# Zeros instead of x1 as the start of the scattered sums, and loads that add in the last norm

## The chip, the cores and the metric

One NeuronCore of one Trainium2 chip runs the whole program. The metric is the device time of one launch in microseconds; several launches are timed and the median is given. One of them was recorded by the hardware profiler.

## The reference

A single decoder layer is applied to 512 prompt tokens and 8 sample tokens (520 rows of 2048 float32 values, computed together). What matters here is the shape of the residual stream:

```python
x = layer_norm(ALPHA * x + mix, ln1_g[l], ln1_b[l])          # called x1 below
ffn = hier_moe(x, w_group[l], b_group[l], w_router[l], b_router[l],
               w_gate[l], w_up[l], w_down[l])
x = layer_norm(ALPHA * x + ffn, ln2_g[l], ln2_b[l])          # the output
...
# hier_moe: best of 4 groups, best 2 of its 4 experts, so two experts of 16 for each token
h = jax.nn.silu(jnp.einsum('td,edf->tef', xf, w_gate)) * jnp.einsum('td,edf->tef', xf, w_up)
y = jnp.einsum('tef,te,efd->td', h, gate.astype(h.dtype), w_down)
```

`mix` is the output of three groups of heads (short convolution, HGRN2 recurrence, windowed attention) behind one input projection and one output projection. An expert has three matrices of 4 MiB each: gate and up of 2048x512, down of 512x2048.

## The kernel before, in words

The program is written engine by engine, each with its own instruction list and explicit semaphores; nothing reorders it. It has these stages, in order of time in the profile:

- **Input projection and heads**, to about 600 us, and **output projection** (16 columns of w_out, `n` in 0 to 15), about 607 to 804 us. SP issues the loads: two 1 MiB buffers (`RAW`) hold weights, ScalarE copies them to a rounded high part (`HI`), GpSimd or VectorE makes the low part (`LO`), TensorE runs three products for each (high x high, low x high, high x low).
- **First norm and routing**, about 804 to 835 us. x1 lies in the tile `R` (104 rows of 5 token tiles, 2048 columns). SP writes it to `x1_rows` in HBM, from which GpSimd gathers the rows of each block of up to 128 (token, expert) pairs. The trace shortens the names `x1_rows` to `x_rows`, `X2` and `X8` to `X`, `LG2` to `LG`, `LB2` to `LB`.
- **Expert blocks**, about 835 to 1456 us. Each block takes 12 weight tiles of 1 MiB: eight for gate and up (`gate_up`, tiles 0 to 7) and four for down (`down`, tiles 8 to 11). SP issues a tile's load into one of six buffers `RAWB` once VectorE has finished the low part (`LOB`) of the tile that had the buffer (semaphores `expert_lo`). ScalarE then makes `HIB`, VectorE `LOB`, TensorE multiplies. The block's result `YO` is scattered by GpSimd to `y_rows` in HBM by an indirect DMA that adds (line 768). The blocks in the middle are a hardware loop on each engine; the first block and the last two stand outside it. In the last block but one, w_down is taken in four columns, and each quarter of `YO` is scattered alone (line 804). The last block's result stays on the chip (`YO2`): TensorE spreads it with 0/1 matrices over the token tiles.
- **Last norm**, from 1455 us. SP waits for the four quarter scatters, loads `y_rows` into `X2` (four tiles of 128 tokens, 1 MiB each, line 707) and the eight sample rows into `X8` (64 KiB, line 709). VectorE adds the spread last block (`added`, line 1767), centres and scales (`centred`, `finished`), ScalarE makes means and squares. The samples go another way through `samples_sum`, `samples_centre` and `samples_finish`, which stand between the tiles in VectorE's list. Tiles 0 and 1 of the output are written by GpSimd DMAs that add to rows already holding the bias (line 817); tiles 2 and 3 and the samples by SP.

`y_rows` must hold x1 before the first block is scattered, so that x1 and all blocks sum there. In the kernel before SP writes the five pieces of `R` to it in the first block's `gate_up`, one between every two weight loads from tile 3 on:

```python
def y_set(i):
    sp.dma_start(y_rows[i * TT:(i + 1) * TT, :], R[:, i, :]).then_inc(s_y0, 16)
...
if isinstance(j, int) and 3 <= i < 3 + NT:
    y_set(i - 3)
```

All loads and stores issued by SP share one hardware DMA queue (q1) and are worked off in the order of issue; GpSimd's go through the software queue (q0). Both use the same 16 DMA engines.

Of the kernel before, what the change touches and what calls it, by code (L numbers as in the profile page):

```python
# [11 lines left out]
ALU = mybir.AluOpType  # L12
# [5 lines left out]
SEQ, DB = 512, 8  # L18
# [24 lines left out]
EARLY = 3  # L43
CHUNKS = list(range(11)) + [12, 13, 11, 14, 15]
# [70 lines left out]
def build(nc, a, o):  # L115
# [149 lines left out]
    with ExitStack() as ctx:  # L265
# [219 lines left out]
        def passed(eng):  # L485

            eng.sem_inc(s_passed, 1)
# [3 lines left out]
        def _(sp):  # L491
# [113 lines left out]
            for n in range(KC):  # L605
# [20 lines left out]
                if n == 0:  # L626
                    sp.dma_start(IOS[0:TT, :], a["ios"]).then_inc(s_rc, 16)
                    sp.dma_start(IOS[TT:128, :], a["ios"][0:128 - TT, :]).then_inc(s_rc, 16)
                if n == 2:
                    sp.wait_ge(s_ob, 2)  # L630
                    sp.wait_ge(s_ym, 2 * EARLY)
                    sp.dma_start(R[0:3, 0:4, 1536:2048], a["ln1g"][0:3, :].rearrange("r (q n) -> r q n", q=4)).then_inc(s_lg, 16)
                    sp.dma_start(R[3:5, 0:4, 1536:2048], a["ln1b"][0:2, :].rearrange("r (q n) -> r q n", q=4)).then_inc(s_lg, 16)
# [24 lines left out]
            def y_set(i):  # L658
                sp.dma_start(y_rows[i * TT:(i + 1) * TT, :], R[:, i, :]).then_inc(s_y0, 16)

            def gate_up(j, m0):
                e = sp.value_load(EBI[0:1, bass.ds(j, 1)], min_val=0, max_val=NE - 1)
                for i in range(8):
                    if isinstance(j, int) and i == 1:
                        x1_out(3)
                        x1_out(4)
                    if isinstance(j, int) and 3 <= i < 3 + NT:
                        y_set(i - 3)
                    bload(i, m0, (a["w_gate"], a["w_up"])[i % 2][bass.ds(e, 1), :, 2048 * (i // 2):2048 * (i // 2) + 2048].rearrange("a p n -> p (a n)"), j)

            def down(j, first, columns=False):
                e = sp.value_load(EBI[0:1, bass.ds(j - 1, 1)], min_val=0, max_val=NE - 1)
                for n in range(4):
                    if columns:
                        w, parts = a["w_down"][bass.ds(e, 1), :, :, 512 * n:512 * n + 512].rearrange("a p c n -> p (a c) n"), 4
                    else:
                        w, parts = a["w_down"][bass.ds(e, 1), :, 2 * (n % 2):2 * (n % 2) + 2, 1024 * (n // 2):1024 * (n // 2) + 1024].rearrange("a p c n -> p (a c) n"), 1
                    i = first + n
                    s = i % NRAW
                    sp.wait_ge(b_lo[(2 + i) % NHL], (2 + i) // NHL + 1 + 4 * (j - 1))  # L680
                    passed(sp)
                    sp.dma_start(RAWB[:, s, :].rearrange("p (c n) -> p c n", c=parts), w).then_inc(b_raw[s], 16)
# [7 lines left out]
            gate_up(nb - 1, 0)  # L690
# [8 lines left out]
            sp.wait_ge(s_y0, 16 * NT)  # L699
# [4 lines left out]
            sp.wait_ge(b_yw, 16 * nb + 48)  # L704
            passed(sp)
            for i in range(NF):
                sp.dma_start(X2[:, i, :], y_rows[128 * i:128 * i + 128, :]).then_inc(f_in[i], 16)
            in8 = "(g r) (c n) -> (r c) g n"
            sp.dma_start(X8[:, :, :], y_rows[SEQ:T, :].rearrange(in8, g=2, c=32)).then_inc(f_in8, 16)
# [3 lines left out]
            sp.wait_ge(f_in8, 32)  # L713
# [13 lines left out]
        def _(pool):  # L727
# [53 lines left out]
            with pool.Fori(1, MAXB) as j:  # L781
                with pool.If(j < last):
# [5 lines left out]
                    pool.wait_ge(s_y0, 16 * NT)  # L788
# [12 lines left out]
            for n in range(4):  # L801
# [5 lines left out]
                    bounds_check=last_quarter, oob_is_err=False, compute_op=ALU.add).then_inc(b_yw, 16)  # L807
            pool.memset(ROWS[:, :], 0.0).then_inc(s_ones, 1)
# [370 lines left out]
        def _(dve):  # L1179
# [282 lines left out]
            lo(NU + 1)  # L1462

# [279 lines left out]
            def samples_sum():  # L1743
                dve.wait_ge(f_in8, 48)
# [622 lines left out]
```

## Time and profile before

| | |
|---|---|
| median of 3 launches | 1496.84 us (1494.42 to 1501.94) |
| profiled execution: device time | 1493.46 us |
| profiled execution: span of its instructions | 1491.6 us |
| mean granted TensorE clock | 0.982 of full speed |
| TensorE matmuls busy | 1439.3 us (96%) |
| VectorE busy | 1015.0 us (68%) |
| ScalarE busy | 770.8 us (52%) |
| GpSimd busy | 190.4 us (13%) |
| DMA moved | 335.36 MB, mean 225 GB/s |
| of it by the software queue q0 | 18.74 MB, 5.0% of 16 engines' span |

Engines are named PE (TensorE matmuls), PEld (its weight loads), DVE (VectorE), ACT (ScalarE), POOL (GpSimd) and SP (SyncE, which only issues DMAs; its queue rows say SPq). A number after L is the line in the kernel. Times of rows are microseconds from the start of the span, durations in "mean ns" nanoseconds.

### The profile page before, as it was taken

Reading aid. Unit: us, or ns where it says so; the run is one execution under the profiler, and the core shown is the slowest. Engines: PE = TensorE matmul, PEld = TensorE weight load, DVE = VectorE, ACT = ScalarE, POOL = GpSimd, SP = SyncE. Lnnn points to the kernel's source line nnn. Section 1 sums busy time; section 2 is a strip of 40 time slices with the busy share of each in tenths; the row PEclk is TensorE's granted clock in tenths of the full one; section 3 lists DMA queues with packets and bytes.
Section 4 is the critical chain, followed back from the end, with each engine's and each line's share of the span. In section 5 each row is a group of like instructions: output and inputs, shape, how many; then the busy total and the mean of one; then the engine's idle time right before and its main releaser. Section 6 shows DMA issues by size and latency. Waiting matters only on the chain.

```text
span 1491.6 us, 24267 instructions
## 1 busy us (share of the span) xinstructions
PE 1439.3 (96%) x9396; PEld 1291.7 (87%) x9396; DVE 1015.0 (68%) x1287; ACT 770.8 (52%) x912; POOL 190.4 (13%) x99
## 2 busy tenths in 40 slices
PE   8999999999999999999997999999999999999995
PEld 7999999999999999999996467888888888888772
DVE  4246746757777787523125668888888888888877
ACT  4245545444434433411110047777777777777774
POOL 0000000000000000234330001121121211222130
PEclk9999999999999999999998899999999999999998
DMA  7321231322213312633435699999999999999997
GB/s 262 123 89 57 86 114 61 96 90 86 88 57 115 116 58 73 205 111 146 145 96 205 207 394 375 384 401 391 392 375 384 384 382 398 387 390 401 348 294 232
DMA packets 74389, 335.36 MB, mean 225 GB/s; under 512 B 12086, under 2 KB 18790, under 8 KB 45514
## 3 DMA queue, kind: packets, MB, share of 16 engines
q1 hardware_dynamic: 68842, 315.54, 56.2%
q0 software_dynamic: 5472, 18.74, 5.0%
q8 instruction: 56, 0.92, 0.2%
q14 instruction: 19, 0.16, 0.0%
HBM read 313.56 MB, written 40.73 MB: 238 GB/s over the span
## 4 chain that ended last, share of the span: by engine, by line
PE 85%; DVE 7%; DMA 3%; ACT 2%; issue 2%; POOL 0%; ACTq 0%; SPq 0%; DVEq 0%; POOLq 0%
PE BANK L1811 13%; PE BANK L1812 13%; PE BANK L1813 13%; PE BANK L2170 7%; PE BANK L2172 7%; PE BANK L2171 7%; PE BANK L2222 4%; PE BANK L2220 4%; PE BANK L2221 4%; PE BANK L2154 2%; DMA RAWB<-in_w_up 2%; PE BANK L2183 2%; PE BANK L1953 1%; PE BANK L1829 1%; PE BANK L2050 1%
## 5 line engine op out<-in xcount | busy, mean ns | idle before, releaser
L1811 PE MATMUL BANK<-XH,HI 128*128 128x260 f32 x1746 | 503.0, 288 | 1.4 <-DVE RT L1487 1.0
L1683 DVE TENSOR_TENSOR LOB<-RAWB,HIB 128x2048 fp32r<-128x2048 f32 x196 | 448.6, 2291 | 74.0 <-ACT HIB L1050 73.1
L1812 PE MATMUL BANK<-XL,HI 128*128 128x260 f32 x1746 | 495.3, 284 | 0.0
L1813 PE MATMUL BANK<-XH,LO 128*128 128x260 f32 x1746 | 494.3, 283 | 0.0
L1050 ACT ACTIVATE HIB<-RAWB 128x2048 fp32r<-128x2048 f32 x196 | 376.4, 1921 | 86.0 <-PE BANK L2172 66.1
L1811 PEld LDWEIGHTS BANK<-XH,HI 128*128 128x128 f32 x1746 | 331.2, 190 | 2.7 <-issue 1.7
L1812 PEld LDWEIGHTS BANK<-XL,HI 128*128 128x128 f32 x1746 | 331.1, 190 | 0.7
L1813 PEld LDWEIGHTS BANK<-XH,LO 128*128 128x128 f32 x1746 | 330.9, 190 | 0.0
L2170 PE MATMUL BANK<-HIB,XGH 128*128 128x512 f32 x512 | 201.8, 394 | 5.5 <-issue 3.0
L2172 PE MATMUL BANK<-LOB,XGH 128*128 128x512 f32 x512 | 200.0, 391 | 0.0
L2171 PE MATMUL BANK<-HIB,XGL 128*128 128x512 f32 x512 | 199.8, 390 | 0.0
L836 ACT ACTIVATE HI<-RAW 128x2048 fp32r<-128x2048 f32 x55 | 105.1, 1911 | 146.5 <-PE BANK L1813 139.6
L731 POOL TENSOR_TENSOR LO<-RAW,HI 128x2048 fp32r<-128x2048 f32 x14 | 66.1, 4721 | 713.5 <-ACT HI L836 713.5
L1198 DVE TENSOR_TENSOR LO<-RAW,HI 128x2048 fp32r<-128x2048 f32 x41 | 93.8, 2289 | 42.9 <-ACT HI L836 42.6
L2170 PEld LDWEIGHTS BANK<-HIB,XGH 128*128 128x128 f32 x512 | 96.7, 189 | 26.2 <-DVE LOB L1683 3.3
L2172 PEld LDWEIGHTS BANK<-LOB,XGH 128*128 128x128 f32 x512 | 96.5, 188 | 20.5
L1487 DVE SCALAR_TENSOR_TENSOR RT<-RT,BANK 128x260 f32<-128x260 f32 x32 | 13.5, 424 | 147.3 <-PE BANK L1813 147.3
L2171 PEld LDWEIGHTS BANK<-HIB,XGL 128*128 128x128 f32 x512 | 96.6, 189 | 19.5
L2220 PE MATMUL BANK<-HIB,HTH 128*128 128x512 f32 x240 | 99.4, 414 | 0.0
L2222 PE MATMUL BANK<-LOB,HTH 128*128 128x512 f32 x240 | 94.7, 395 | 0.0
L2221 PE MATMUL BANK<-HIB,HTL 128*128 128x512 f32 x240 | 93.6, 390 | 0.0
L768 POOL DMA_INDIRECT y_rows<-YO,YIXC x15 | 37.4, 2495 | 355.3 <-ACT YO L1071 355.3
(388 smaller groups left out, 1674.5 us busy)
## 6 DMA issues: line engine op xcount, KB each, us to landing
RAWB<-in_w_down SPq DMA_DIRECT2D x68, 1024.0 KB, 9.5
RAWB<-in_w_gate SPq DMA_DIRECT2D x67, 1024.0 KB, 9.4
RAWB<-in_w_up SPq DMA_DIRECT2D x67, 1024.0 KB, 8.9
RAW<-in_w_in SPq DMA_DIRECT2D x39, 1024.0 KB, 4.9
RAW<-in_w_out SPq DMA_DIRECT2D x16, 1024.0 KB, 5.0
Y<-in_xT SPq DMA_DIRECT2D x8, 520.0 KB, 9.1
RT<-in_xT SPq DMA_DIRECT2D x16, 260.0 KB, 5.2
x_rows<-R SPq DMA_DIRECT2D x5, 832.0 KB
```

What stands on the lines that cost most here:

```text
L836: act.activation(HI[:, u % 2, :], RAW[:, u % 2, :], ACT.Copy).then_inc(s_hi, 1)
L1050: act.activation(HIB[:, s, :], RAWB[:, r, :], ACT.Copy).then_inc(b_hi, 1)
L1683: dve.tensor_tensor(LOB[:, s, :], RAWB[:, r, :], HIB[:, s, :].bitcast(F32), ALU.subtract).then_inc(b_lo[s], 1)
L1811: pe.matmul(bank, hw[:, c, :], h, start=(c == 0), stop=False)
L1812: pe.matmul(bank, hw[:, c, :], l, start=False, stop=False)
L1813: ins = pe.matmul(bank, lw[:, c, :], h, start=False, stop=(c == KC - 1))
L2170: pe.matmul(b, XGH[:, cc, :], hw[:, c, :], start=(cc == 0), stop=False)
L2171: pe.matmul(b, XGL[:, cc, :], hw[:, c, :], start=False, stop=False)
L2172: ins = pe.matmul(b, XGH[:, cc, :], lw[:, c, :], start=False, stop=(cc == KC - 1))
L2220: pe.matmul(b, th[:, c, :], hw[:, m, :], start=(c == 0), stop=False)
L2221: pe.matmul(b, tl[:, c, :], hw[:, m, :], start=False, stop=False)
L2222: ins = pe.matmul(b, th[:, c, :], lw[:, m, :], start=False, stop=(c == 3))
```

## The change

Five things change.

1. `y_rows` starts at zero. VectorE clears the tile `NDIST` (128x256, no longer used by then) at the start of the output projection, and SP writes it, repeated eight times along a row, to the five pieces of `y_rows` at n = 3, 4, 8, 12 and 13. The five writes of x1 in the first block go.
2. In the last `gate_up` SP loads x1 from `x1_rows` into `X2`, one tile of 1 MiB before weight tiles 0, 2, 4 and 6, and after tile 7 the sample rows into `X8`.
3. After the quarter scatters GpSimd, no longer SP, issues the loads of `y_rows` into `X2` and `X8`, now as DMAs that add to what is there.
4. Waits follow: scatters wait for the zeros, `samples_sum` for the adding load of `X8`.
5. The w_down loads that are not in columns name their destination as 2 pieces of 1024 instead of 1 of 2048.

```diff
+ZEROED = (3, 4, 8, 12, 13)
...
+                if n in ZEROED:
+                    i = ZEROED.index(n)
+                    sp.wait_ge(s_y0, 1)
+                    sp.dma_start(y_rows[i * TT:(i + 1) * TT, :].rearrange("p (k c) -> p k c", c=256),
+                                 NDIST[0:TT, :].unsqueeze(1).to_broadcast([TT, 8, 256])).then_inc(s_y0, 16)
...
-            def y_set(i):
-                sp.dma_start(y_rows[i * TT:(i + 1) * TT, :], R[:, i, :]).then_inc(s_y0, 16)
-
-            def gate_up(j, m0):
+            def x1_in(i):
+                if i == 0:
+                    sp.wait_ge(s_x1w, 16 * (5 + NT))
+                sp.dma_start(X2[:, i, :], x1_rows[128 * i:128 * i + 128, :]).then_inc(s_y0, 16)
+
+            def gate_up(j, m0, fill=False):
...
-                    if isinstance(j, int) and 3 <= i < 3 + NT:
-                        y_set(i - 3)
+                    if fill and i % 2 == 0:
+                        x1_in(i // 2)
...
-                        w, parts = a["w_down"][bass.ds(e, 1), :, 2 * (n % 2):2 * (n % 2) + 2, 1024 * (n // 2):1024 * (n // 2) + 1024].rearrange("a p c n -> p (a c) n"), 1
+                        w, parts = a["w_down"][bass.ds(e, 1), :, 2 * (n % 2):2 * (n % 2) + 2, 1024 * (n // 2):1024 * (n // 2) + 1024].rearrange("a p c n -> p (a c) n"), 2
...
-            gate_up(nb - 1, 0)
+            gate_up(nb - 1, 0, True)
+            sp.dma_start(X8[:, :, :], x1_rows[SEQ:T, :].rearrange(in8, g=2, c=32)).then_inc(s_y0, 16)
             down(nb - 1, 8, True)
             down(nb, 0, True)
...
-            sp.wait_ge(s_y0, 16 * NT)
...
-            sp.wait_ge(b_yw, 16 * nb + 48)
-            passed(sp)
-            for i in range(NF):
-                sp.dma_start(X2[:, i, :], y_rows[128 * i:128 * i + 128, :]).then_inc(f_in[i], 16)
-            in8 = "(g r) (c n) -> (r c) g n"
-            sp.dma_start(X8[:, :, :], y_rows[SEQ:T, :].rearrange(in8, g=2, c=32)).then_inc(f_in8, 16)
...
-            sp.wait_ge(f_in8, 32)
+            sp.wait_ge(f_in8, 16)
...
-                    pool.wait_ge(s_y0, 16 * NT)
+                    pool.wait_ge(s_y0, 1 + 16 * NT)
...
+            pool.wait_ge(b_yw, 16 * nb + 48)
+            passed(pool)
+            pool.wait_ge(s_y0, 1 + 16 * (NT + NF + 1))
+            pool.wait_ge(b_xg, 16 * last)
+            passed(pool)
+            for i in range(NF):
+                pool.dma_start(out=X2[:, i, :], in_=y_rows[128 * i:128 * i + 128, :], accum_op=ALU.add).then_inc(f_in[i], 16)
+            pool.dma_start(out=X8[:, :, :], in_=y_rows[SEQ:T, :].rearrange(in8, g=2, c=32), accum_op=ALU.add).then_inc(b_xg, 16)
             pool.memset(ROWS[:, :], 0.0).then_inc(s_ones, 1)
...
             lo(NU + 1)
+            dve.memset(NDIST[:, :], 0.0).then_inc(s_y0, 1)
...
             def samples_sum():
-                dve.wait_ge(f_in8, 48)
+                dve.wait_ge(f_in8, 32)
+                dve.wait_ge(b_xg, 16 * nb)
```

How the program's order moves is seen at two places. The first is SP's list in the last `gate_up`, outside the loop; the kernel before:

```order
L662 TENSOR_LOAD EBI
L662 ISA x2
L600 ISA
L602 ISA [waits expert_lo2]
L602 DMA RAWB<-in_w_gate 128x2048
L600 REGISTER_ALU
L602 DMA RAWB<-in_w_up 128x2048 [waits expert_lo0]
L602 ISA [waits expert_lo1]
L602 DMA RAWB<-in_w_gate 128x2048
```

and the changed one (X2 is the tile of the last norm, the names carry the changed kernel's lines):

```order
L672 ISA x2
L669 DMA X2_118<-x1_rows 128x2048 [waits x1_out]
L601 ISA
L603 ISA [waits expert_lo2]
L603 DMA RAWB_94<-in_w_gate 128x2048
L601 REGISTER_ALU
L603 DMA RAWB_94<-in_w_up 128x2048 [waits expert_lo0]
L669 DMA X2_118<-x1_rows 128x2048
L603 ISA [waits expert_lo1]
L603 DMA RAWB_94<-in_w_gate 128x2048
```

A load of x1 now stands in SP's queue ahead of weight tile 0 and ahead of tile 2, and two more ahead of tiles 4 and 6.

The second is GpSimd's list behind the quarter scatters, the kernel before:

```order
L804 DMA y_rows<-YO,YIX_171 2080x512 [waits down_copied]
L808 MEMSET ROWS 128x128
L811 MEMSET ROWS 32x32 [waits ones_set]
L811 MEMSET ROWS 32x32 x3
L817 DMA out_yp<-YA 128x2048 [waits tokens_in,y_scaled,y_out]
L817 DMA out_yp<-YA 128x2048 [waits y_scaled]
```

and the changed one:

```order
L808 DMA y_rows<-YO,YIX4_171 2080x512 [waits down_copied]
L813 ISA
L819 DMA X2_118<-y_rows 128x2048 [waits block_out,y_rows_set,tokens_in]
L819 DMA X2_118<-y_rows 128x2048 x3
L820 DMA X8_119<-y_rows 128x2x64
L821 MEMSET ROWS_123 128x128
L824 MEMSET ROWS_123 32x32 [waits ones_set]
L824 MEMSET ROWS_123 32x32 x3
L830 DMA out_yp<-YA_111 128x2048 [waits tokens_in,y_scaled,y_out]
```

Five DMAs come into GpSimd's list between the last scatter and the clearing of `ROWS`, and stand in the software queue ahead of the two output writes.

## Rows read from the trace of the kernel before

**Rows 1.** The page's chain that ended last: share of the span by engine.
```profile
PE 85%; DVE 7%; DMA 3%; ACT 2%; issue 2%; POOL 0%; ACTq 0%; SPq 0%; DVEq 0%; POOLq 0%
```

**Rows 2.** Stages: length, busy of PE, PEld, DVE, ACT, POOL; clock, DMA share, GB/s.
```profile
740.00:760.00 20.00, 20.00 (x171) 20.00 (x170) 5.12 (x10) 1.92 (x1) 9.02 (x2) 1.00 0.28 96
855.00:870.00 15.00, 15.00 (x33) 5.59 (x32) 8.89 (x6) 5.37 (x4) 0.00 (x0) 1.00 1.02 399
1000.00:1100.00 100.00, 100.00 (x469) 83.55 (x469) 88.65 (x53) 79.14 (x65) 17.19 (x11) 1.00 1.00 385
1405.00:1410.00 5.00, 2.03 (x12) 1.62 (x10) 3.13 (x3) 4.88 (x5) 0.00 (x0) 1.00 0.86 306
1410.00:1415.00 5.00, 5.00 (x22) 4.13 (x23) 2.97 (x3) 2.04 (x2) 0.00 (x0) 1.00 0.80 311
1415.00:1420.00 5.00, 5.00 (x23) 4.13 (x22) 4.50 (x2) 3.87 (x3) 2.50 (x1) 1.00 0.81 248
```

**Rows 3.** SP's queue in the first block: start, us, what it issued.
```profile
868.03 0.55 SPq L659 DMA_DIRECT2D y_rows<-R  x1
869.77 0.34 SPq L602 DMA_DIRECT2D RAWB<-in_w_up  x1
```

**Rows 4.** ScalarE and TensorE in the first block: start, us, what, idle before.
```profile
894.02 1.92 ACT L1050 ACTIVATE HIB<-RAWB 128x2048 fp32r<-128x2048 f32 x1 [3.13 <-DMA RAWB<-in_w_up]
...
898.32 0.50 PE L2170 MATMUL BANK<-HIB,XGH 128*128 128x512 f32 x1 [1.28 <-DVE LOB L1683]
```

**Rows 5.** TensorE at 608 us, and VectorE's clearing of a 128x512 tile.
```profile
607.89 0.36 PE L1811 MATMUL BANK<-XH,HI 128*128 128x260 f32 x1 [1.03 <-DVE RT L1487]
...
L1302 DVE MEMSET SF<- 128x512 f32 x4 | 1.9, 485 | 0.6 <-DVE PR L1387 0.5
```

**Rows 6.** SP's queue in the last gate_up: tiles 0, 3, 5, 6, 7 and 8.
```profile
1390.11 0.35 SPq L602 DMA_DIRECT2D RAWB<-in_w_gate  x1
...
1395.30 0.33 SPq L602 DMA_DIRECT2D RAWB<-in_w_up  x1
...
1402.18 0.33 SPq L602 DMA_DIRECT2D RAWB<-in_w_up  x1
1405.52 0.33 SPq L602 DMA_DIRECT2D RAWB<-in_w_gate  x1
1409.45 0.33 SPq L602 DMA_DIRECT2D RAWB<-in_w_up  x1
1414.41 21.17 SPq L682 DMA_DIRECT2D RAWB<-in_w_down  x8
```

**Rows 7.** DMA issues of 1395-1396, 1402-1403, 1416-1419: count, size, us to landing.
```profile
RAWB<-in_w_up SPq DMA_DIRECT2D x1, 1024.0 KB, 8.4
...
RAWB<-in_w_up SPq DMA_DIRECT2D x1, 1024.0 KB, 6.9
...
RAWB<-in_w_down SPq DMA_DIRECT2D x1, 1024.0 KB, 7.7
```

**Rows 8.** ScalarE in the last gate_up: tiles 2, 5, 6, and 7 to 9.
```profile
1407.46 1.93 ACT L1050 ACTIVATE HIB<-RAWB 128x2048 fp32r<-128x2048 f32 x1
...
1418.40 1.92 ACT L1050 ACTIVATE HIB<-RAWB 128x2048 fp32r<-128x2048 f32 x1 [0.80 <-PE BANK L2172]
1421.18 1.92 ACT L1050 ACTIVATE HIB<-RAWB 128x2048 fp32r<-128x2048 f32 x1 [0.86 <-PE BANK L2172]
1426.16 5.53 ACT L1050 ACTIVATE HIB<-RAWB 128x2048 fp32r<-128x2048 f32 x3 [3.06 <-issue]
```

**Rows 9.** The chain of waits at the end: start, us, what.
```profile
1446.28 8.68 DMA y_rows<-YO,YIX
...
1455.04 4.85 DMA X<-y_rows
1459.92 2.53 DVE X L1767 x8
...
1473.01 0.30 DVE X L1745
...
1487.31 0.29 DVE Q L1760
```

**Rows 10.** DMA queues in 1473-1481.8 and 1460-1463: packets, MB, share of 16 engines.
```profile
q0 software_dynamic: 189, 1.42, 89.0%
...
q1 hardware_dynamic: 175, 1.30, 102.7%
```

**Rows 11.** GpSimd's first adding write of the output.
```profile
1473.00 0.93 POOL L817 DMA_DIRECT2D out_yp<-YA  x1 [23.75 <-ACT YA L1161]
```

**Rows 12.** GB/s in 40 equal slices of 1473 to 1475 us.
```profile
GB/s 0 0 0 0 0 0 0 0 0 0 0 0 0 0 0 0 0 0 0 0 0 0 0 0 0 0 0 0 0 164 983 983 328 164 0 0 0 0 0 0
```

More of the change, by code:

```diff
@@ L656, in _ @@
                 x1_out(i)
-            def y_set(i):
-                sp.dma_start(y_rows[i * TT:(i + 1) * TT, :], R[:, i, :]).then_inc(s_y0, 16)
-            def gate_up(j, m0):
+            in8 = "(g r) (c n) -> (r c) g n"
+            def x1_in(i):
[3 more added lines that the diff above has]
+            def gate_up(j, m0, fill=False):
                 e = sp.value_load(EBI[0:1, bass.ds(j, 1)], min_val=0, max_val=NE - 1)
@@ L807, in _ @@
                     bounds_check=last_quarter, oob_is_err=False, compute_op=ALU.add).then_inc(b_yw, 16)
+            in8 = "(g r) (c n) -> (r c) g n"
+            pool.wait_ge(b_yw, 16 * nb + 48)
[6 more added lines that the diff above has]
+            pool.dma_start(out=X8[:, :, :], in_=y_rows[SEQ:T, :].rearrange(in8, g=2, c=32), accum_op=ALU.add).then_inc(b_xg, 16)
             pool.memset(ROWS[:, :], 0.0).then_inc(s_ones, 1)
```

## The prediction

> **What bounds the kernel now.** I read the page's chain first [rows 1]: TensorE holds 85% of it, VectorE 7%, DMA 3%. A change that touches neither TensorE's list nor its operands can only act where TensorE or the last norm waits. Then the table of stages [rows 2]. In the middle expert blocks (1000 to 1100) TensorE is busy 100.00 of 100 us while the DMA share is 1.00 at 385 GB/s: TensorE sets the pace, but the DMA engines have next to nothing to spare, so bytes put into or taken out of the expert stage matter at its ends, where TensorE has gaps. In the output projection (740 to 760) the share is 0.28 at 96 GB/s, so there is room. Then the queues and engines at three places: the first block, the last `gate_up`, and the end.
>
> In the first block the DMA engines are full (share 1.02 at 399 GB/s in 855 to 870 [rows 2]). The last x1 write to `y_rows` is issued at 868.03 and tile 7 right after, at 869.77 [rows 3]. ScalarE waits 3.13 us for that tile, until 894.02, and TensorE in turn stands 1.28 us before 898.32 [rows 4]. That is all the time TensorE loses there to the DMA queue. At the end the chain is: last quarter scatter 8.68 us, first load of `y_rows` 4.85 us, then VectorE nearly without a break from 1459.92 to 1487.6, then the last store [rows 9].
>
> **The change part by part.** Times are of the profiled execution: span 1491.6, device time 1493.5 us, 3.4 us under the median of 1496.84 (all three launches lie within 1494.4 to 1501.9). I add the sum to both.
>
> *x1 writes of the first block go.* Five writes, 520 x 8 KB = 4.26 MB. At 399 GB/s [rows 2] that is 10.7 us of queue ahead of tile 7. The tile would land about 11 us earlier, well before ScalarE wants it, and the 1.28 us gap closes. Nothing behind it gains more, since TensorE has no idle time in the blocks that follow. The first scatter also need not wait for them, but it waits for the block's result anyway. Gain 1.3 us, at least 1.0. The other end is a case in which the whole 10.7 us comes back; it is a rival below.
>
> *Zeros.* The memset of `NDIST` stands in VectorE's list just ahead of the residual addition for which TensorE waits 1.03 us until 607.89 [rows 5]. A 128x512 memset took 485 ns, so half of that size is about 0.24 us, and I put it on the path: +0.2, bounds 0 and 0.5. The five writes cover again 4.26 MB, in 1 KB pieces, in a stage where the engines are busy 0.28 of the time [rows 2]: 4.26 MB at half of 399 GB/s would be 21 us spread over 120 us or more. TensorE is busy 20.00 of 20 us there, so its weight tiles come in time, and I take 0; if that cover failed, one late weight tile would cost about 3 us.
>
> *x1 loads in the last block.* Four tiles of 1 MiB come into SP's queue ahead of weight tiles 0, 2, 4 and 6, and 64 KB behind tile 7. Two landings give the pace of the queue: tile 3 was issued at 1395.30 and took 8.4 us, tile 5 at 1402.18 and took 6.9 [rows 6, 7]: they land at 1403.7 and 1409.1, so 2.7 us for each tile. Tiles 0 and 1 then land 2.7 us later, 2 and 3 5.4, 4 and 5 8.1, 6 and 7 10.8. Against that stands how early they are now. Tile 2 lands near 1401.0 and is used at 1407.46, 6.5 us of slack against 5.4. Tile 5 has 1418.40 - 1409.1 = 9.3 against 8.1 [rows 8]. Tile 6 follows tile 5 by two tiles in the new queue (one of x1, its own): 1409.1 + 8.1 + 5.4 = 1422.6, and it is used at 1421.18, so 1.4 us late. The wait is not made up, because ScalarE then leaves its loop with 3.06 us of its own ("issue") before tile 7 at 1426.16 [rows 8], and that tile is what TensorE waits for. The w_down tiles inherit what is left of the 10.8 us. The engines were idle for 0.14, 0.20 and 0.19 of three stretches of 5 us [rows 2], 2.7 us in all, so 8.1 us is left. A w_down tile issued about 1417.4 took 7.7 us, to 1425.1 [rows 7], and was used as the third of ScalarE's row at about 1429.8 [rows 8]: 4.7 us of slack, plus the 1.4 already lost, so about 2 us more. These overlap in part; I take +2.5 us for TensorE's end. Bounds: 0 (all hidden) and 10.8 (nothing hidden); I hold to the low side because each slack was read off.
>
> *The quarter scatters* run while SP's queue still works off that backlog; now the last takes 8.68 us [rows 9] beside the gamma and beta loads, which come later in the changed kernel. +0.5, bounds 0 and 3.
>
> *Adding loads.* The load of `y_rows` moves to GpSimd. SP issued 0.08 us after the scatter landed (1446.28 + 8.68, to 1455.04) [rows 9]; GpSimd has two more waits to pass and an issue of 0.93 us [rows 11], of which +0.4 shows. The rate matters more. The trace has a direct DMA that adds only in the other direction, from SBUF to HBM (line 817). Issued at 1473.00 [rows 11], its first packets are in the 30th of 40 slices of 0.05 us, at 1474.45 [rows 12], and alone in the machine until SP's first store at 1481.8 it moved 1.42 MB [rows 10]: 193 GB/s, 5.4 us for 1 MiB. Plain loads into `X2` moved 1.30 MB in 3 us at a share of 1.03 [rows 10]: 422 GB/s of full engines, 2.5 us for 1 MiB. So an adding load into SBUF costs between 2.5 and 5.8 us a tile (1.42 MB over 0.89 of 8.8 us gives the 5.8); the nearest row is the adding one and I take 5.4. The first plain tile landed 4.85 us after its issue [rows 9], 2.4 more than its 2.5 of moving. Adding tiles then land 2.4 + 5.4 = 7.8, 13.2, 18.6 and 24.0 us after the first issue, and the 64 KB of samples, in 256-byte pieces, about 2 us later, 26. Before, VectorE started tile 0 at 4.9, tile 1 at 10.1, the sample sum at 1473.01 - 1455.04 = 18.0. Now tile 0 starts 2.9 us late, tile 2 5.7 late, and `samples_sum`, which stands ahead of tile 3 in VectorE's list, 8.0 late. Everything behind it (tile 3, three centrings, two finishes, the samples' finish, the last store) follows it without slack. So +8.0, bounds 0 and 9.5. GpSimd's own adding stores stand in q0 behind these loads: 26 + 2 x 5.4 = 37 after the issue, and the end is then at 36.6 + 8, so they are covered.
>
> The Trainium skill bears on the direction that no row has. "Collectives: The Full Stack", section "The bandwidth ceiling: the fold count and why AG ≠ RS ≠ AR", says that a DMA that adds is slower not for the adding but because it must read two sources for one write, and gives a ratio of 1.93. That holds for any direction, so it speaks against plain speed here. By that rule a tile would take 1.93 x 2.5 = 4.8 us as an estimate and the sample sum would start 5.6 us late instead of 8.0, the whole 2.4 us sooner than my sum. This trace has 5.4 / 2.5 = 2.2 for writes to HBM [rows 10], and nothing for loads.
>
> *w_down's two pieces.* The source was two pieces of 1024 per partition already; the loads lie in blocks where TensorE is never idle [rows 2]. 0.
>
> Sum: -1.3 + 0.2 + 2.5 + 0.5 + 0.4 + 8.0 = +10.3 us. Profiled device time 1503.8, median 1507.
>
> **The rivals.** (a) *Adding loads run at the plain pace.* At 2.5 us a tile they land at 4.9, 7.4, 9.9 and 12.4, the samples before 15, all ahead of VectorE's 18.0; the 8.0 goes to 0 and the sum is +2.3: 1499, no measurable change. For it: a write into SBUF has no HBM row to read back. Against it: each byte is still read twice. It decides at 18.0 = 2.4 + 4t + 2, that is t = 3.4 us a tile; above that the end moves. (b) *The x1 loads are not hidden at all.* Tiles 6 and 7 late by their full 10.8 us: 8.3 more than I count, 1515. For it: share 1.00 in the loop and no spare for the first tiles. Against it: the 6.5 and 9.3 us of slack. (c) *The start gives back all it carried.* If the 10.7 us of writes held the whole expert stage back, taking them out would give 10.7, and with plain-speed loads the sum is 2.3 - (10.7 - 1.3) = -7.1, with the last block hidden too -9.6: 1488. Against it: TensorE's 100% in rows 2, which leaves an earlier DMA nothing to bring forward. (d) *The zero writes hold up SP.* Pieces of 1 KB at n = 12 and 13 delay a w_out tile or the first expert tiles: 3 us on top, 1510.
>
> **How the numbers follow.** Chances: forecast 0.53, (a) 0.27, (b) 0.11, (c) 0.05, (d) 0.04. A measurement of this kernel tells about 0.5%, 7.5 us, from no change, so the line is at 1504.3. The forecast's own range is 1501 to 1511: with 4.8 us a tile and TensorE's delay at 1 it falls just under the line; I count 0.1 of its 0.53 as the same. (b) and (d) are slower. So slower 0.58, same 0.37, faster 0.05. The range runs from (a) with the last block hidden, 1497, to (b), 1515.
>
> **What would show it.** In the profile after: no wait of ScalarE for tile 7 and no TensorE gap near 896 (else the first step is wrong); a DMA share over 1 in the last `gate_up`, ScalarE starting tile 6 one to three us late and TensorE's end two to three us later relative to its start of that block; the first adding load landing nearly 8 us after its issue, and VectorE idle before tile 2 and above all before the sample sum. If VectorE goes from tile 0 to tile 3 without waits for DMA, the forecast is wrong and (a) is right. If TensorE is idle in the middle blocks, either kernel's DMA pace decides and I misread the stage.

## The result and the profile after

| | before | changed |
|---|---|---|
| median of 9 launches each | 1496.85 us (1493.87 to 1501.94) | 1503.57 us (1499.88 to 1506.92) |
| ratio, 95% interval | | 1.0044 [1.0032, 1.0056] |
| profiled span | 1491.6 us | 1501.4 us |
| mean granted TensorE clock | 0.982 | 0.981 |

The changed kernel is 6.6 us slower (4.8 to 8.4). The profiled pair differs by 9.8 us, so some of what one pair of traces shows is not the change; the experiments below take the parts one by one.

The chain by engine, from the page of the changed kernel:

```profile
PE 84%; DVE 7%; DMA 4%; ACT 3%; issue 2%; POOL 0%; ACTq 0%; POOLq 0%; SPq 0%; DVEq 0%
```

Against [rows 1] TensorE's share is down by one point and DMA's and ScalarE's are up by one each. One point is 15 us, so this only says that some waiting came in. The queues, from the same page:

```profile
DMA packets 78878, 339.62 MB, mean 226 GB/s; under 512 B 12423, under 2 KB 23287, under 8 KB 50011
...
q0 software_dynamic: 6320, 23.00, 6.4%
```

The kernel moves 4.26 MB more in all (335.36 before): the x1 loads. It moves 4.26 MB more in the software queue (18.74 before): the loads that went over to GpSimd.

**The start.** VectorE and TensorE at 609 us, timeline of the changed kernel (start, us, engine, what, in brackets the idle time before and who ended it):

```profile
606.97 2.28 DVE L1211 TENSOR_TENSOR LO<-RAW,HI 128x2048 fp32r<-128x2048 f32 x1
609.26 0.27 DVE L1476 MEMSET NDIST<- 128x256 f32 x1
609.85 0.76 DVE L1501 SCALAR_TENSOR_TENSOR RT<-RT,BANK 128x260 f32<-128x260 f32 x2
...
610.42 0.36 PE L1826 MATMUL BANK<-XH,HI 128*128 128x260 f32 x1 [1.27 <-DVE RT L1501]
```

TensorE's wait for the residual addition is 1.27 us where it was 1.03 [rows 5]: the memset costs 0.24. The addition itself is 2.53 us later than before, but VectorE's item ahead of the memset is already 2.3 us later, so that part is from before the change. The stages of the changed kernel, with the zeros in flight in the first two rows (length, busy PE, PEld, DVE, ACT, POOL; clock, DMA share, GB/s):

```profile
600.00:700.00 100.00, 98.73 (x825) 98.55 (x824) 32.88 (x58) 24.21 (x23) 33.95 (x7) 0.98 0.56 189
700.00:800.00 100.00, 100.00 (x859) 100.00 (x858) 23.60 (x46) 13.42 (x7) 32.14 (x7) 1.00 0.40 132
...
880.00:885.00 5.00, 5.00 (x23) 4.11 (x22) 3.62 (x3) 3.56 (x3) 0.00 (x0) 1.00 0.52 166
```

The same two windows of the kernel before:

```profile
600.00:700.00 100.00, 98.97 (x828) 98.80 (x827) 30.98 (x54) 23.82 (x22) 33.95 (x7) 0.98 0.49 171
700.00:800.00 100.00, 100.00 (x863) 100.00 (x861) 23.17 (x45) 11.52 (x7) 32.14 (x7) 1.00 0.33 111
```

The zeros raise the DMA share from 0.49 and 0.33 to 0.56 and 0.40 and TensorE still has all of 100 us in the second window. In the first block the pressure is gone: the share is 0.52 at 880 to 885, where it was 0.94. ScalarE there, timeline after:

```profile
890.30 1.92 ACT L1063 ACTIVATE HIB<-RAWB 128x2048 fp32r<-128x2048 f32 x1 [0.80 <-PE BANK L2187]
...
895.68 1.92 ACT L1063 ACTIVATE HIB<-RAWB 128x2048 fp32r<-128x2048 f32 x1 [0.80 <-PE BANK L2187]
...
901.13 0.60 ACT L1072 ACTIVATE SG<-BANK 128x512 f32<-128x512 f32 x1 [0.81 <-PE BANK L2187]
```

It waits for TensorE now and no longer 3.13 us for a load [rows 4]. From the residual addition (`RT`, near 608 us, just behind the memset) to the silu `SG` near 901 us the changed kernel takes 901.13 - 609.85 = 291.3 us, the kernel before 294.1. I call this the start stretch.

**The last gate_up**, windows of the changed kernel:

```profile
1405.00:1410.00 5.00, 2.15 (x12) 1.68 (x10) 3.35 (x3) 5.00 (x6) 0.00 (x0) 1.00 1.01 421
1410.00:1415.00 5.00, 4.88 (x14) 3.90 (x15) 2.89 (x2) 0.60 (x2) 0.00 (x0) 0.66 1.02 424
1415.00:1420.00 5.00, 5.00 (x23) 4.13 (x22) 2.83 (x2) 3.82 (x3) 2.28 (x1) 1.00 1.01 423
```

The DMA share is 1.01 to 1.02 where it was 0.80 to 0.86 [rows 2]: the x1 loads fill the gaps. ScalarE and TensorE in it:

```profile
1410.12 0.49 PE L2185 MATMUL BANK<-HIB,XGH 128*128 128x512 f32 x1 [2.97 <-issue]
...
1414.50 1.92 ACT L1063 ACTIVATE HIB<-RAWB 128x2048 fp32r<-128x2048 f32 x1 [4.40 <-PE BANK L2187]
...
1423.01 1.92 ACT L1063 ACTIVATE HIB<-RAWB 128x2048 fp32r<-128x2048 f32 x1 [0.86 <-PE BANK L2187]
1427.99 5.52 ACT L1063 ACTIVATE HIB<-RAWB 128x2048 fp32r<-128x2048 f32 x3 [3.06 <-issue]
```

Every wait of ScalarE ends on TensorE or on its own sequence, none on a load. It starts tile 6 at 1423.01, against 1421.18 [rows 8], 1.83 us later, though the block started only 0.2 us later. The delay is there already at tile 3 (4.40 us of waiting for TensorE) and belongs to the granted clock of 0.66 in 1410 to 1415, which was 1.00 in the profile before: 0.34 of 5 us is 1.7 us lost for TensorE.

**The last norm**, timeline of GpSimd and VectorE after:

```profile
1458.60 3.56 POOL L819 DMA_DIRECT2D X<-y_rows  x4 [8.43 <-DMA y_rows<-YO,YIX]
1460.86 2.55 POOL L820 DMA_DIRECT2D X<-y_rows  x1
...
1466.66 0.69 DVE L1782 SCALAR_TENSOR_TENSOR X<-X,BANK 128x512 f32<-128x512 f32 x1 [11.34 <-DMA X<-y_rows]
1477.35 0.69 DVE L1782 SCALAR_TENSOR_TENSOR X<-X,BANK 128x512 f32<-128x512 f32 x1 [2.87 <-DMA X<-y_rows]
1484.31 0.29 DVE L1760 TENSOR_TENSOR X<-X,W 128x128 f32<-128x128 f32 x1 [2.10 <-DMA W<-z_rows]
```

and the DMAs in the chain that ended last (start, us, what):

```profile
1448.13 9.74 DMA y_rows<-YO,YIX
1458.60 8.03 DMA X<-y_rows
1471.51 8.22 DMA z_rows<-Z
1479.74 4.45 DMA W<-z_rows
```

Counted from the first issue at 1458.60, tile 0 starts at 8.1 us, tile 2 at 18.75, the sample sum at 25.7. In the profile before these were 4.9, 12.9 and 18.0 ([rows 9], and for tile 2 this line of the same chain), and VectorE went from tile to tile:

```profile
1467.98 2.53 DVE X L1767 x8
```

The whole tail, first issue to the end of the span, is 42.8 us, against 1491.6 - 1455.04 = 36.6 [rows 9]. DMA queues of 1466 to 1475, after (packets, MB, share of 16 engines):

```profile
DMA packets 261, 1.95 MB, mean 217 GB/s; under 512 B 23, under 2 KB 23, under 8 KB 23
...
q0 software_dynamic: 261, 1.95, 104.8%
```

and of 1456 to 1466 before, where the plain loads run:

```profile
DMA packets 535, 3.99 MB, mean 399 GB/s; under 512 B 48, under 2 KB 48, under 8 KB 48
...
q1 hardware_dynamic: 535, 3.99, 99.4%
```

Both fill the engines: the adding loads at 217 GB/s (187 in 1460 to 1466, at a share of 0.98), the plain ones at 399.

The 9.8 us of this pair lie at these places:

- The last `gate_up` starts 0.2 us later. 2.3 us were lost ahead of the first changed instruction and 0.2 at the memset; the rest was recovered in between.
- From there to the issue of the fourth quarter scatter: +1.6, its low clock.
- That scatter takes 9.74 us and not 8.68: +1.1.
- From its landing to the first issue it is 0.73 us and not 0.08: +0.65.
- The tail: +6.2.

### The profile page after: what moved, and what is told of

Its sections match the earlier page's. It is cut to its first block, busy times and chain, and to the rows that moved or that the text cites. A ratio compares the mean times of both kernels' runs of the same rounds, so it can differ in the third digit from the quotient of the medians.

```text
span 1501.4 us, 24275 instructions
## 1 busy us (share of the span) xinstructions
PE 1440.4 (96%) x9396; PEld 1292.4 (86%) x9396; DVE 1015.7 (68%) x1288; ACT 771.3 (51%) x912; POOL 195.2 (13%) x104
## 4 chain that ended last, share of the span: by engine, by line
PE 84%; DVE 7%; DMA 4%; ACT 3%; issue 2%; POOL 0%; ACTq 0%; POOLq 0%; SPq 0%; DVEq 0%
PE BANK L1826 12%; PE BANK L1827 12%; PE BANK L1828 12%; PE BANK L2185 7%; PE BANK L2187 7%; PE BANK L2186 7%; PE BANK L2237 4%; PE BANK L2235 4%; PE BANK L2236 4%; PE BANK L2169 2%; PE BANK L2198 2%; PE BANK L1968 1%; PE BANK L1844 1%; PE BANK L2065 1%; ACT SC L906 1%
```

## The experiments

Intervals are 95%, ratios always to the kernel before, whose median stayed between 1496.9 and 1498.5 us in all comparisons. "tail" and "start stretch" are measured as above; "PE stretch" is from TensorE's first matmul of the last `gate_up` to the issue of the fourth quarter scatter (before 36.4, changed 38.0 us).

**Zeros alone.** The kernel before, with the first part of the change only. Nothing loads x1 in its place, so x1 is missing from the last norm's input.

```diff
+                if n in ZEROED:
...
+                    sp.dma_start(y_rows[i * TT:(i + 1) * TT, :].rearrange("p (k c) -> p k c", c=256),
+                                 NDIST[0:TT, :].unsqueeze(1).to_broadcast([TT, 8, 256])).then_inc(s_y0, 16)
...
-                    if isinstance(j, int) and 3 <= i < 3 + NT:
-                        y_set(i - 3)
```

> Only the start of the change: zeros written during the output projection, the five x1 writes of the first block gone; no x1 loads, plain loads as before, so x1 is missing from the last norm's input. Theory P (the adding loads are the loss, the x1 writes cost only the gap at tile 7): 0.2 for the memset less 1.3 for the gap, so about 1 us faster than before, ratio 0.999; in the profile no TensorE gap near 896. Rival S (the x1 writes hold the whole expert stage back, and the change's loss at the end is far larger than its net): 5 to 10 us faster, ratio 0.994 to 0.997. Rival C (TensorE's clock drop in the first block comes from these writes): the drop after the block's start is gone in this profile, 1.5 us more.

Ratio 0.9982 [0.9968, 0.9995]: 2.7 us faster. No gap of TensorE is left in 880 to 905; start stretch 293.1 us in a trace with a clock of 0.94 and 0.97 in 860 to 900, so a low clock in the first block does not need the x1 writes. Tail 36.6, as before. Taking the x1 writes out gives more than the 1.1 us that the traced gap promised (1.3 less 0.2 for the memset), and far less than 10.7. The low clock at 1410 to 1415 is here too, without any x1 load:

```profile
1410.00:1415.00 5.00, 4.43 (x13) 3.63 (x14) 2.89 (x2) 0.51 (x2) 0.00 (x0) 0.66 0.76 264
```

**x1 loads alone.** The kernel before, with x1 loaded in the last `gate_up` and then overwritten by the plain loads.

```diff
+                    if fill and i % 2 == 0:
+                        x1_in(i // 2)
...
-            gate_up(nb - 1, 0)
+            gate_up(nb - 1, 0, True)
+            sp.dma_start(X8[:, :, :], x1_rows[SEQ:T, :].rearrange(in8, g=2, c=32)).then_inc(s_y0, 16)
```

> The kernel before plus the x1 loads of the last gate_up and nothing else (the plain loads of y_rows overwrite them later): the result is as before. Theory P: DMA share goes to 1.0 in 1405 to 1420, ScalarE waits for no tile, TensorE's end is unmoved; the last quarter scatter lands up to 1 us later; 0 to 1 us slower, ratio 1.000 to 1.001. Rival Q (the queue's backlog reaches TensorE): 2.5 us or more slower, ratio 1.002 or more, with ScalarE idle on DMA RAWB at tiles 6 to 9. Rival C2 (the fuller DMA queue brings the clock drop at the last block): a granted clock below 1 in 1410 to 1415.

Ratio 1.0019 [1.0008, 1.0031], profiled span 1503.5. But the trace puts nearly all of its extra time ahead of the place that was edited: start stretch 302.2 us against 294.1, with two gaps of TensorE:

```profile
900.45 0.50 PE L2180 MATMUL BANK<-HIB,XGH 128*128 128x512 f32 x1 [1.71 <-DVE LOB L1693]
905.46 0.50 PE L2180 MATMUL BANK<-HIB,XGH 128*128 128x512 f32 x1 [1.98 <-DVE LOB L1693]
```

and low clocks earlier, in stages where TensorE never stood, as in this window:

```profile
700.00:720.00 20.00, 20.00 (x154) 20.00 (x153) 7.29 (x13) 3.11 (x2) 4.59 (x1) 0.83 0.22 80
```

In the last `gate_up` the share is 1.00 to 1.02, ScalarE waits for no load, and the PE stretch is 38.0. Tail 36.8. The edit's own cost cannot be read from one trace like this; a second one follows below.

**Adding loads on top.** As above, with the five loads made adding ones of GpSimd. The sums in the last norm hold x1 twice.

```diff
-            for i in range(NF):
-                sp.dma_start(X2[:, i, :], y_rows[128 * i:128 * i + 128, :]).then_inc(f_in[i], 16)
...
+            for i in range(NF):
+                pool.dma_start(out=X2[:, i, :], in_=y_rows[128 * i:128 * i + 128, :], accum_op=ALU.add).then_inc(f_in[i], 16)
```

> e2 plus the adding loads issued by GpSimd, with the x1 writes of the first block kept (x1 is counted twice in the last norm's input). Theory P: 6 to 8 us slower than e2, so ratio 1.004 to 1.006 over before; the first adding load lands 8 us after its issue, the sample sum starts about 26 us after it. Rival R (the pace of the loads does not matter, the loss is in the queue ahead of them): within 1 us of e2.

Ratio 1.0058 [1.0044, 1.0071], so 0.0039 or 5.8 us over x1 loads alone in the same comparison. VectorE's waits:

```profile
1475.09 0.69 DVE L1782 SCALAR_TENSOR_TENSOR X<-X,BANK 128x512 f32<-128x512 f32 x1 [11.14 <-DMA X<-y_rows]
1487.00 0.69 DVE L1782 SCALAR_TENSOR_TENSOR X<-X,BANK 128x512 f32<-128x512 f32 x1 [4.09 <-DMA X<-y_rows]
1492.90 0.29 DVE L1760 TENSOR_TENSOR X<-X,W 128x128 f32<-128x128 f32 x1 [1.04 <-DMA X<-y_rows]
```

From the issue at 1467.05: 8.0, 19.95 and 25.85 us. Tail 42.95. Tile 0 and the samples come as in the changed kernel and tile 2 1.2 us later, with another start of the sums: the pace belongs to the kind of DMA.

**Plain loads by GpSimd.** The changed kernel, with `accum_op` taken from the five loads; the last norm then lacks x1.

```diff
-                pool.dma_start(out=X2[:, i, :], in_=y_rows[128 * i:128 * i + 128, :], accum_op=ALU.add).then_inc(f_in[i], 16)
+                pool.dma_start(out=X2[:, i, :], in_=y_rows[128 * i:128 * i + 128, :]).then_inc(f_in[i], 16)
```

> The changed kernel with the five loads of y_rows made plain, still issued by GpSimd (they overwrite x1, which is missing from the last norm's input). Theory P: the loads land at 2.5 us a tile, VectorE waits only for the first, and the kernel is about 6 us faster than the changed one: -1.3 + 0.2 + 0 to 1 + 0.6 for the issue, ratio 0.999 to 1.001 over before. Rival I (issue from GpSimd through the software queue is what costs, not the adding): the loads still land 15 us and more after issue, ratio 1.003 to 1.004.

Ratio 0.9997 [0.9984, 1.0010]. GpSimd and VectorE in it:

```profile
1458.53 2.23 POOL L819 DMA_DIRECT2D X<-y_rows  x4 [8.51 <-DMA y_rows<-YO,YIX]
...
1463.64 0.69 DVE L1782 SCALAR_TENSOR_TENSOR X<-X,BANK 128x512 f32<-128x512 f32 x1 [8.48 <-DMA X<-y_rows]
```

Tile 0 starts 5.1 us after the issue and the tail is 36.7, so the one argument `accum_op` of five DMAs carries 42.8 - 36.7 = 6.1 us by the traces and 0.0047 x 1497 = 7.0 us by the launches. Issue by GpSimd costs about 0.9: the issue comes 0.75 us after the scatter's landing (0.08 by SP) and the first load lands in 5.09 us (4.85). PE stretch 37.8, scatter 9.80 us.

**The kernel before against itself**, and **x1 loads again.** The kernel before and the kernel of "x1 loads alone" once more, with nothing changed.

> The kernel before, unchanged, timed against itself. All theories expect a ratio of 1.000 within 0.001; its width is what the others are read against. Theory K (the stretches of TensorE at its lower clock fall by the program's own course): its profile has the drops where the profile of before has them, in 860 to 880 and not in 1400 to 1420. Rival L (they fall by chance): a drop of the same length stands in another stage.

> e2 unchanged, a second time. In its first profile TensorE had further stretches at a lower clock in 700 to 720 and 900 to 920, hundreds of microseconds ahead of the only edit, and the kernel was 2.8 us slower. Theory K (by the program's course): the same two stretches again, ratio 1.002. Rival L (by chance): they are gone in this profile, ratio 1.000 to 1.001, since the x1 loads themselves cost TensorE nothing.

Ratios 0.9999 [0.9982, 1.0017] and 1.0004 [0.9989, 1.0019]. The new trace of the kernel before spans 1500.2 us, 8.6 more than the first, and has the gaps that the first lacked:

```profile
896.34 0.50 PE L2170 MATMUL BANK<-HIB,XGH 128*128 128x512 f32 x1 [1.80 <-DVE LOB L1683]
901.39 0.50 PE L2170 MATMUL BANK<-HIB,XGH 128*128 128x512 f32 x1 [2.03 <-DVE LOB L1683]
...
906.05 0.60 ACT L1059 ACTIVATE SG<-BANK 128x512 f32<-128x512 f32 x1 [2.02 <-PE BANK L2172]
```

Its start stretch is 297.4 us; x1 loads again has 296.9. And its clock has a low stretch where the first trace had none, and a longer one (windows):

```profile
900.00:905.00 5.00, 3.61 (x10) 2.86 (x11) 4.57 (x3) 3.41 (x2) 0.00 (x0) 0.73 0.97 387
...
1415.00:1420.00 5.00, 4.67 (x11) 3.71 (x12) 2.89 (x2) 0.32 (x1) 0.00 (x0) 0.50 0.83 308
```

So the first trace of the kernel before, on which the prediction rests, was one of its better executions: 294.1 us where the other four traces with the x1 writes at their old place (this one, the two of x1 loads, and x1 loads with adding loads) have 296.9 to 302.2. Its PE stretch was 36.4, and this second one's, under the longer low stretch, 39.1, with no x1 loads in either. The mean of the two comparisons for x1 loads is 1.0012, about 1.7 us, and one interval holds 1.

**x1 writes later.** The kernel before with its five writes moved behind the `w_down` loads, one before them and one after each of the four.

```diff
-                    if isinstance(j, int) and 3 <= i < 3 + NT:
-                        y_set(i - 3)
...
+                    if isinstance(j, int):
+                        y_set(n + 1)
...
+            y_set(0)
```

> The kernel before with its five x1 writes moved behind tile 7: one ahead of the first w_down tile, one behind each of the four. No zeros, no x1 loads, plain loads. Theory P (the writes cost only because they stand ahead of tiles that TensorE is about to want, and the engines are idle for 3 to 4 us in 880 to 890 without them): the gap at 896 goes and no new one of that size comes, 1 to 2 us faster, ratio 0.999. Rival M (the engines have no room anywhere in the first two blocks): the same gap comes back at the w_down tiles or in the second block, ratio 1.000 to 1.001.

Ratio 1.0000 [0.9982, 1.0017]. The gap at 896 goes, and the start stretch is 291.3 us, as in the changed kernel. But the block's scatter, which waits for the five writes, and the gather behind it are later: GpSimd's first item after that wait starts at 906.59 after 29.85 us of idling (891.86 before), and TensorE pays:

```profile
906.59 1.12 POOL L764 COPY YIXC<-YIX 128x1 int32 x1 [29.85 <-DMA y_rows<-R]
...
914.10 0.79 PE L2171 MATMUL BANK<-HIB,XGH 128*128 128x512 f32 x1 [2.74 <-DVE XGL L1694]
```

The gain is given back 13 us later. The writes cost something at both places tried in the full stage, and nothing was seen of them in the output projection.

**Samples behind tile 3.** The changed kernel with the sample sum moved behind the addition of tile 3 and the centring of tile 2.

```diff
+            added(3)
+            centred(2)
             samples_sum()
-            added(3)
+            finished(2, 1)
             samples_centre()
-            centred(2)
-            finished(2, 1)
```

> The changed kernel with the sample sum moved in VectorE's list from ahead of tile 3 to behind tile 3 and its centring. Theory P (the adding loads set the pace, the sample sum is only the last to come): VectorE starts tile 3 when it lands, 24 us after the first issue instead of 26.2, about 2 us faster than the changed kernel, ratio 1.002 to 1.004 over before. Rival W (the samples' own way, the write and read of the 64 KB of z_rows beside the adding loads, is what holds the end): the end comes with the samples and nothing is gained, or 1 us is lost.

Ratio 1.0034 [1.0019, 1.0049], tail 42.3 us. Tile 3 now starts 25.2 us after the first issue (at 1456.36), as soon as it has landed and no longer behind the samples (26.25 in the changed kernel):

```profile
1481.56 0.69 DVE L1782 SCALAR_TENSOR_TENSOR X<-X,BANK 128x512 f32<-128x512 f32 x1 [0.23 <-DMA X<-y_rows]
```

About 2 us were expected from the new order. It is worth 0.5 us of the 6.2 by the tails; by the launches the interval overlaps that of the changed kernel, so no gain is shown there. What binds is the pace of the four tiles: tile 3 lands 25 us after the issue and not 24.

**Half and half.** Zeros, x1 loads and adding loads only for tiles 2 and 3. Tiles 0 and 1 and the samples start from x1 and are loaded plainly by SP, so that VectorE has work while the adding loads run. Of the x1 writes 2.2 MB stay in the first block. Nothing is left out of the computation. The edit is shown against the changed kernel; w_down's loads name one piece here, as in the kernel before.

```diff
-ZEROED = (3, 4, 8, 12, 13)
+ZEROED = (3, 8)
...
-                    if fill and i % 2 == 0:
-                        x1_in(i // 2)
+                    if isinstance(j, int) and 3 <= i < 7:
+                        y_set(i - 3)
+                    if fill and i in (2, 4):
+                        x1_in(1 + i // 2)
...
+            for i in range(2):
+                sp.dma_start(X2[:, i, :], y_rows[128 * i:128 * i + 128, :]).then_inc(f_in[i], 16)
...
-            for i in range(NF):
+            for i in range(2, NF):
                 pool.dma_start(out=X2[:, i, :], in_=y_rows[128 * i:128 * i + 128, :], accum_op=ALU.add).then_inc(f_in[i], 16)
```

> A version of full result: only rows 256 to 511 of y_rows start at zero (tiles 2 and 3 of the last norm, x1 loaded into their place in the last gate_up, y added onto it by two GpSimd loads); rows 0 to 255 and the samples start at x1, written in the first block as before but 2.2 MB instead of 4.3, and are loaded plainly by SP. Theory P: VectorE wants tile 2 about 13 us and tile 3 about 18.5 us after the first load; two plain and two adding tiles land at about 13 and 18.5, so the end is lost by at most 1 us, and half of the writes ahead of tile 7 (5 us of queue) is enough to lose the gap at 896: 1 to 2.5 us faster than the kernel before, ratio 0.998 to 0.9995. Rival T (adding loads slow the plain loads beside them, and the sum is no better): VectorE waits for tile 1 or 3 by 2 us or more and the ratio is 1.000 to 1.002.

Ratio 1.0001 [0.9988, 1.0013]. The DMAs in its chain:

```profile
1458.05 5.10 DMA X<-y_rows
...
1468.02 8.52 DMA z_rows<-Z
1476.56 1.87 DMA W<-z_rows
```

and VectorE's waits:

```profile
1470.51 0.69 DVE L1790 SCALAR_TENSOR_TENSOR X<-X,BANK 128x512 f32<-128x512 f32 x1 [2.02 <-DMA X<-y_rows]
1478.46 0.29 DVE L1768 TENSOR_TENSOR X<-X,W 128x128 f32<-128x128 f32 x1 [0.27 <-DMA W<-z_rows]
```

VectorE waits for no load of tile 2 any more. But it now waits 2.0 us for plain tile 1, which runs beside the adding loads of the other queue. Behind that it waits 0.3 us for the samples, whose 64 KB write takes 8.5 us. The tail is 39.05, 2.5 us over that of the kernel before, which uses up what the start stretch of 291.3 gained.

**Three repeats**: half and half, zeros alone, and the changed kernel, with nothing changed.

> The same kernel a second time, since the width of one comparison is as large as the effect. Theory P: ratio 0.998 to 0.9995. Rival T: 1.000 to 1.002.

> e1 a second time (zero start alone, x1 missing from the last norm's input). Revised theory P2 (in the usual execution the x1 writes of the first block cost TensorE two gaps and not the one of the first profile): 3 us faster than the kernel before, ratio 0.998, no gap before 900. First theory: 1 us faster, ratio 0.999.

> The changed kernel a second time. Theory P2: 3 lost at the adding loads' 6 to 7 less 3 at the start and about 1 for the queue's last loads and the issue: ratio 1.003 to 1.005; first adding tile 8 us after its issue, sample sum 26 after it, and in the last block a TensorE that waits for no weight tile. Rival: these were of one execution, and the landings move by more than 1 us.

Ratios 0.9990 [0.9976, 1.0004], 0.9975 [0.9963, 0.9987] and 1.0042 [1.0027, 1.0058]. Tails 38.9, 36.7 and 42.9 us. Start stretches 293.3, 292.7 and 291.6. Half and half beats the changed kernel by some 7 us (means of two, 0.9996 and 1.0043), with intervals apart; against the kernel before it is not shown to differ. No version that computes everything was shown to beat the kernel before.

## Why the prediction was right, and where its sizes were not

The forecast was +10.3 us, a slower kernel because of the pace of the adding loads, and the launches say +6.6. The sign and the main cause were right; nearly every size was off, mostly towards too slow. Point by point:

| step | forecast | measured |
|---|---|---|
| x1 writes go | -1.3 | with the memset: -2.7 and -3.7 by launches (zeros alone, twice) |
| memset of the zeros | +0.2 | +0.24 (TensorE's wait 1.03 to 1.27) |
| the zeros' DMAs | 0 | 0 (TensorE 100.00 of 100 us at a share of 0.40) |
| x1 loads delay TensorE | +2.5 | no wait seen; by launches +1.7 as a mean, once not told from 0 |
| quarter scatter beside them | +0.5 | not resolved: 8.5 to 9.9 us in kernels with and without x1 loads |
| GpSimd starts the loads | +0.4 | +0.9 (0.67 to the issue, 0.24 in the landing) |
| adding loads | +8.0 | 6.1 by tails, 7.0 and 5.8 by launches |

*The adding loads, right in mechanism.* 7.8, 18.6 and 26 us from the issue were forecast for tile 0, tile 2 and the samples; 8.1, 18.75 and 25.7 were seen, and the wait stands where the prediction put it, before tile 2 and before the sample sum. Leaving out `accum_op` alone takes it away. The pace was taken from a row of the other direction, adding stores to HBM (5.4 us a tile), and comes near for loads: tile 2 lands 10.7 us after tile 0 here, 5.35 us a tile, and 11.9 in three other traces, 5.9 a tile. Against the 2.5 of plain loads that is 2.1 to 2.4 times as long; by the throughput of full engines the ratio is 1.8 to 2.1 (399 over 217 and 187 GB/s). The Trainium skill, "Collectives: The Full Stack", section "The bandwidth ceiling: the fold count and why AG ≠ RS ≠ AR", gives two reads for a write and a ratio of 1.93 for the adding step of a ring collective. The throughput measured here agrees with that ratio, the landings lie above it. The term itself was 1 to 2 us too large: `samples_sum` is late by 25.7 - 18.0 = 7.7 as forecast, but that is not all handed on to the end. From VectorE's last item to the end of the span the changed kernel takes 1501.4 - 1498.9 = 2.5 us and the kernel before 1491.6 - 1487.6 = 4.0: the sample store landed in 2.1 us there and in 3.6 before, where it stood with more stores under way (SP's two 512 KB stores landed in a median of 4.2 us before and 2.8 after). The step that let everything behind the sample sum, the last store too, follow it without slack was wrong by these 1.5 us.

*The start, too small.* "Gain 1.3 us" was read off one gap in one trace. That trace was one of the better executions. The other trace of the same kernel has two gaps, of 1.8 and 2.0 us, the three others with the x1 writes at their old place have two of 0.9 to 2.0, and a low clock may follow. The bound given, "at least 1.0", held; the size was half or less of what was measured. The reading that nothing beyond the gaps comes back was right: some 3 us and not 10.7.

*The last block, too large.* The prediction let tile 6 land 1.4 us late and stacked 8.1 us of backlog behind it. No wait of ScalarE for a load in this block appeared in any of the nine traces that have x1 loads there (two of them with half of the loads), though the engines ran full as forecast. The landings show the step that was too large. Tile 5 was to land at 1417.2; in the changed kernel it was issued at 1402.39 and took 13.1 us, so it landed at 1415.5. Tile 6's landing is on record in plain loads by GpSimd, first its issue and the time to landing, then ScalarE's start on it:

```profile
RAWB<-in_w_gate SPq DMA_DIRECT2D x1, 1024.0 KB, 15.0
...
1422.87 1.92 ACT L1063 ACTIVATE HIB<-RAWB 128x2048 fp32r<-128x2048 f32 x1 [0.86 <-PE BANK L2187]
```

Issued at 1406.10, it landed at 1421.1, 1.8 us before it was used. Most of that margin comes from the low clock, which holds TensorE and with it ScalarE back. At full clock, in the kernel before, ScalarE took tile 6 11.3 us after TensorE's first product of the block (1421.18 - 1409.90). Here the tile landed 10.9 us after it (1421.1 - 1410.18), in x1 loads alone and with adding loads on top 11.1 and 11.2. So at full clock it would have been in time by 0.1 to 0.4 us, as an estimate: hidden, but barely. The pace is the reason. From tile 2's landing at 1406.2 to tile 5's at 1416.1 four tiles pass, 2.5 us each, where the prediction took 2.7 from two landings of a queue that was not always full.

The sign given in advance, "ScalarE starting tile 6 one to three us late", appeared at 1.8, and would have been taken for a hit. It was luck: the clock did it, and the same loss is in the two runs of zeros alone and in x1 writes later (PE stretch 37.8 to 38.0), which have no x1 load. That the launches put +1.7 us on the x1 loads, near the +2.5 forecast, does not make the step right either, since the wait that was to cause it is in no trace.

*The rivals.* (a), plain pace: refuted by the landings and by plain loads by GpSimd. (b), x1 loads not hidden: refuted, no wait. (c), the start gives back all: refuted, a third of it came (its 1488 is 1487 by its own sum). (d), zero writes hold SP up: refuted; from the residual addition to the first norm's transposes it is 197.6 us in both kernels (807.45 - 609.85 and 804.92 - 607.32).

The sum with what was measured in place of what was forecast: -3.2 (start and memset), +1.7 (x1 loads), +0.9 (GpSimd), +6.3 (adding loads, mean of three), 5.7 in all, against 6.6 [4.8, 8.4]. What stays open: by launches, the changed kernel less its adding loads (plain loads by GpSimd, 0.9997) is 2.2 to 3.3 us behind zeros alone (0.9982 and 0.9975). GpSimd's issue is 0.9 of it. The other 1 to 2 us may lie in the x1 loads, in the scatter beside them, or in w_down's two pieces, forecast at 0 and tried in no run alone; no trace shows a wait for any of them. The two pieces touch all expert blocks. From the silu near 901 us to the first product of the last `gate_up` the traces with them take 508.8 to 509.0 us, and 510.9 in plain loads by GpSimd. Those with one piece take 508.5 to 509.4, and 510.9 in one of half and half (x1 writes later is left out: its scatter stands in that stretch). That speaks against a cost of the pieces and does not settle it.

## What to carry to other kernels

In this kernel DMAs that add ran at about half the pace of plain loads, into SBUF (5.35 to 6.0 us for 1 MiB) as into HBM (5.4), against 2.5. So one may save a vector addition only where nobody waits for it. At the end of a program it stretches the last load chain by its own extra time, and here a small plain DMA beside it became slow too. Bytes moved out of a stage with full DMA engines into one with idle ones were worth the waits that they had caused, here 3 us for 4.3 MB, and not their transfer time; moved within the full stage they gained nothing (ratio 1.0000). Before a term of one or two microseconds is read off a trace, look at a second trace of the same kernel: here two of them differ by 8.6 us. And a sign named in advance should be one that only the named cause can give.

## What the runs showed of the hardware

- An adding DMA into SBUF: 5.35 to 6.0 us for 1 MiB in rows of 8 KB, all 16 engines busy at 187 to 217 GB/s; plain about 2.5 us, 399 to 424 GB/s. GpSimd spends 3.56 us on the issue of four such loads and 2.23 on four plain ones; for the piece with 256-byte elements 2.55 against 0.73.
- Small plain DMAs are slow beside them. The 64 KB write of `z_rows` takes 1479.74 - 1471.51 = 8.2 us in the changed kernel and 7.2 to 8.5 in the other five traces with adding loads. In the eight without them it takes 2.8 to 3.4, and 3.4 with plain loads by GpSimd in the same software queue. In the changed kernel it ends the sample sum's wait together with the adding load of `X8`.
- The granted clock falls to its lower level (1.2 of 2.4 GHz; 0.50 over a whole window of 5 us in the second trace of the kernel before) for some microseconds. A mean of 0.66 over 5 us, as in 1410 to 1415 of the changed kernel, is worth 1.7 us of TensorE. The falls lie at other places in executions of one unchanged kernel: 875 to 880 in the first trace of the kernel before, 900 to 905 and 1415 to 1420 in the second. In the expert stage TensorE had been idle in part just before (3.30 busy of 5.00 us in 870 to 875, 2.15 of 5.00 in 1405 to 1410 of the changed kernel). But in the first trace of the kernel before it was as idle in 1405 to 1410 (2.03 of 5.00) and the clock stayed at 1.00. In the output projection of x1 loads alone it had been busy throughout, and the clock fell all the same. So no edit is needed to move the falls; whether an edit can move them as well was not settled. x1 loads again had kept the one between 700 and 720 and lost that at 900 to 920.
